# Gate columns of the second block's memory folded into the first values tiles, and the tiles beside the second attention moved up one unit

## The reference, cut to what matters

```
h = modulate(rms_norm_2(x, norm_mix_g), sh1, sc1)
proj = h @ w_in                                   # 1024 x 2832
q_a, k_a, v_a, qk_m, v_m, o_m, gates = split(proj)  # 512, 128, 128, 1024, 512, 512, 16 columns
y_attn = axial_gqa_attention(q_a, k_a, v_a, ...)    # 8 heads, softmax over all 512 keys
qk = silu(conv5(qk_m));  q, k = split(qk)
g = (gates + gate_b).reshape(B, S, 4, 4)            # input and forget gates, forward and backward
h_fw, h_bw = mlstm(q, k, v_m, i, log_sigmoid(f))    # one pass forward, one over the flipped tokens
y_mem = norm(h_fw + h_bw) * norm_g * sigmoid(o_m)
x = x + g1 * concat(y_attn, y_mem) @ w_out
```

## Time and profile before

| | |
|---|---|
| median of 3 runs | 1550.72 us (1549.45 to 1551.03) |
| the profiled execution's own time | 1549.7 us |
| its span, first to last instruction | 1547.9 us |
| PE busy | 1500.0 us (97%), 11612 matmuls |
| PEld, DVE, ACT, POOL busy | 86%, 66%, 42%, 2% |
| mean granted TensorE clock | 0.995 |

### The profile page before, as it was taken

How to read it: one execution, slowest core, us unless ns; L and a number is a source line. 1 busy time by engine, 2 the same in 40 slices (tenths; PEclk the granted TensorE clock), 3 DMA queues, 4 the chain that set the end, 5 groups by cost and what they waited for, 6 DMA issues and landing times.

```text
span 1547.9 us, 27582 instructions
## 1 busy us (share of the span) xinstructions
PE 1500.0 (97%) x11612; PEld 1326.0 (86%) x11612; DVE 1024.9 (66%) x1441; ACT 655.4 (42%) x1052; POOL 23.2 (2%) x20
## 2 busy tenths in 40 slices
PE   7999999999998999999999899999989999999998
PEld 7988878888998999999887667767767999998876
DVE  5533446785446877777656766676688888885454
ACT  5433343433334222122343545546645555554343
POOL 0000000000000000000000011000000000000000
PEclk9999999999999999999999999999999999999999
DMA  5221104452231333332445213110013233222222
GB/s 182 83 83 55 42 3 153 153 173 95 95 109 70 103 137 103 115 124 76 137 148 166 96 49 109 55 35 28 28 55 109 82 110 110 95 98 82 95 95 82
DMA packets 37707, 147.72 MB, mean 95 GB/s; under 512 B 4305, under 2 KB 4433, under 8 KB 27857
## 3 DMA queue, kind: packets, MB, share of 16 engines
q1 hardware_dynamic: 36288, 142.76, 27.2%
q10 hardware_dynamic: 1152, 2.16, 0.4%
q0 software_dynamic: 144, 1.05, 0.2%
HBM read 143.86 MB, written 2.10 MB: 94 GB/s over the span
## 4 chain that ended last, share of the span: by engine, by line
PE 85%; DVE 8%; ACT 4%; issue 2%; ACTq 0%; POOL 0%; DVEq 0%
PE ps L567 19%; PE ps L569 18%; PE ps L568 18%; PE ps L1489 4%; PE ps L1487 4%; PE ps L1488 4%; ACT t L1540 1%; DVE t L2265 1%; PE ps L603 1%; PE ps L604 1%; PE ps L605 1%; PE ps L751 1%; PE ps L1193 1%; PE ps L729 1%; PE ps L1162 1%
## 5 line engine op out<-in xcount | busy, mean ns | idle before, releaser
L567 PE MATMUL ps<-t 128*128 128x258 f32 (+4 forms) x2160 | 688.9, 319 | 23.1 <-DVE t L2313 8.7
L569 PE MATMUL ps<-t 128*128 128x258 f32 (+4 forms) x2160 | 677.2, 313 | 0.0
L568 PE MATMUL ps<-t 128*128 128x258 f32 (+4 forms) x2160 | 675.7, 313 | 0.0
L567 PEld LDWEIGHTS ps<-t 128*128 128x128 f32 (+1 forms) x2160 | 407.3, 189 | 67.4 <-issue 16.8
L569 PEld LDWEIGHTS ps<-t 128*128 128x128 f32 (+1 forms) x2160 | 407.0, 188 | 27.3
L568 PEld LDWEIGHTS ps<-t 128*128 128x128 f32 (+1 forms) x2160 | 407.7, 189 | 23.8
L2265 DVE TENSOR_TENSOR t<-t 128x1024 fp32r<-128x1024 f32 (+2 forms) x121 | 205.6, 1700 | 204.3 <-ACT t L1540 204.2
L1540 ACT ACTIVATE t<-t 128x1024 fp32r<-128x1024 f32 (+2 forms) x121 | 174.0, 1438 | 186.7 <-PE ps L569 173.6
L1489 PE MATMUL ps<-t 128*128 128x256 f32 x504 | 142.6, 283 | 0.0
L1487 PE MATMUL ps<-t 128*128 128x256 f32 x504 | 142.5, 283 | 0.1
L1488 PE MATMUL ps<-t 128*128 128x256 f32 x504 | 141.3, 280 | 0.0
(11 more groups left out here) (324 smaller groups left out, 1785.2 us busy)
## 6 DMA issues: line engine op xcount, KB each, us to landing
t<-in_W SPq DMA_DIRECT2D x75, 1024.0 KB, 4.8
t<-in_W SPq DMA_DIRECT2D x62, 512.0 KB, 3.6
t<-in_W SPq DMA_DIRECT2D x100, 256.0 KB, 4.0
t<-in_W SPq DMA_DIRECT2D x4, 644.0 KB, 3.8
t<-in_XT ACTq DMA_DIRECT2D x8, 264.0 KB, 7.5
out<-t SPq DMA_DIRECT2D x8, 256.0 KB, 2.7
t<-in_ROPE POOLq DMA_DIRECT2D x1, 1024.0 KB, 5.2
t<-in_CONS SPq DMA_DIRECT2D x1, 423.0 KB, 11.3
```

What stands on the lines that cost most here:

```text
L567: pe.matmul(out, wh, xh, start=first, stop=False)
L568: pe.matmul(out, wh, xl, start=False, stop=False)
L569: return pe.matmul(out, wl, xh, start=False, stop=last)
```

## The change

The gates' weight chunk goes. Their 16 columns stand in the first two values chunks (338 columns for 322), so that `v5_first` leaves them, token-major, at columns 322 to 337 of banks 0 to 3. `evac_v5(0, t)` copies them with one more operation into `gtok`, a tile of 4 x 128 columns that GpSimd has zeroed, 4 columns at 0, 32, 64 and 96 of each 128. A new `gate_turn` in unit 0 transposes the four into bank 0, where the gate tile stood before.

Unit u now computes tile f = u+1, and unit 16 none. ScalarE's and VectorE's work on the tiles and the splits are one unit earlier: splits in even units up to 12, the convolution in units 5 to 12. `gate_rows` stays in units 1 to 5, `gate_columns`, `gcol` and `ncol` in unit 8, the steps on `mrow` in units 2, 6 and 7; the columns go through bank 0, and tile f = 10 waits for them.

```diff
-ORDER += [("q2", 0), ("kq", 0), ("q3", 0), ("v5", 0), ("v5", 1), ("gt2", 0), ("o2", 0), ("o2", 1)]
+ORDER += [("q2", 0), ("kq", 0), ("q3", 0), ("v5", 0), ("v5", 1), ("o2", 0), ("o2", 1)]
...
+        gtok = mb[0][:, :].rearrange("p (t n) -> p t n", t=4)
...
         def gq_split(u):
-            return AT["o2", 0] + (0 if u == 0 else (u + 1) // 2) if u == 0 or (u % 2 == 1 and u <= 13) else None
+            return AT["o2", 1] + u // 2 if u % 2 == 0 and u <= 12 else None
...
+        def gates_of(t):
+            return bank(t, 16, off=322).rearrange("p (g c) -> p g c", g=4)
+
+        def gate_slots(t):
+            return gtok[:, t, :].rearrange("p (g c) -> p g c", g=4)[:, :, 0:4]
...
             po.dma_start(rope[:, :, :], ROPE).then_inc(S["d_rope"], 16)
+            po.memset(mb[0][:, :], 0.0).then_inc(S["half"], 1)
...
-                    out, a = bank(t, 322), slice(128 * t, 128 * t + 128)
+                    out, a = bank(t, 338), slice(128 * t, 128 * t + 128)
...
                 if part == 0:
-                    if f == 0:
-                        pe.wait_ge(S["ev_v5_d"], 1)
-                    elif f == 1:
+                    if f == 1:
                         pe.wait_ge(S["ev_v5_a"], 1)
                     elif f == 2:
                         pe.wait_ge(S["gt_a"], 1)
...
-                    if f == 9:
+                    if f == 10:
                         pe.wait_ge(S["gt_d"], 6)
                         pe.wait_ge(S["gt_a"], 5)
...
+            def gate_turn():
+                pe.wait_ge(S["ev_v5_a"], 2)
+                pe.wait_ge(S["ev_v5_d"], 2)
+                for t in range(4):
+                    ins = pe.transpose(bank(0, P, off=128 * t), gtok[:, t, :], C("id"))
+                ins.then_inc(S["mm_gt"], 1)
 
             def gate_columns():
-                pe.wait_ge(S["cv_c"], 3)
+                pe.wait_ge(S["cv_c"], 4)
...
-                            ins = pe.transpose(bank(1, 4, off=c0 + 16 * d + 4 * i), rw[:, 128 * i:128 * i + 128],
+                            ins = pe.transpose(bank(0, 4, off=c0 + 16 * d + 4 * i), rw[:, 128 * i:128 * i + 128],
...
             for u in range(17):
                 if u < 15:
                     gqa_scores(u + 1)
-                beside_attention(u, 0)
                 if u < 16:
+                    beside_attention(u + 1, 0)
                     gqa_turn(u, 0)
+                if u == 0:
+                    gate_turn()
                 if u >= 1:
                     gqa_values(u - 1)
-                beside_attention(u, 1)
                 if u < 16:
+                    beside_attention(u + 1, 1)
                     gqa_turn(u, 1)
...
@@ ScalarE
+                    if c == 0:
+                        ac.wait_ge(S["half"], 2)
+                        ac.activation(gate_slots(t), gates_of(t), ACT.Copy)
...
-            split(AT["gt2", 0])
+            split(AT["o2", 0])
...
+                if u == 1:
+                    beside_attention(0)
                 if u >= 1:
-                    beside_attention(u - 1)
-                if u == 13:
+                    beside_attention(u)
+                if u == 12:
                     split(gq_split(u))
                 if u < 15:
                     gqa_exp(u + 1)
-                if gq_split(u) is not None and u != 13:
+                if gq_split(u) is not None and u != 12:
                     split(gq_split(u))
...
-                if u == 16:
-                    beside_attention(16)
@@ VectorE
+                    if c == 0:
+                        dv.wait_ge(S["half"], 2)
+                        dv.tensor_copy(gate_slots(t), gates_of(t))
...
-            split(AT["gt2", 0])
+            split(AT["o2", 0])
...
-                if u == 5:
+                if u == 4:
                     dv.wait_ge(S["r_y"], 15)
                     for i in range(2):
                         dv.memset(cv[i], 0.0).then_inc(S["cv_z"], 1)
-                if 6 <= u <= 13:
-                    evac_conv(u - 6)
-                if 14 <= u:
-                    evac_v5(1, u - 14)
+                if 5 <= u <= 12:
+                    evac_conv(u - 5)
+                if 13 <= u:
+                    evac_v5(1, u - 13)
...
-                    dv.tensor_copy(gcol[:, :], bank(1, 32)).then_inc(S["gt_d"], 6)
+                    dv.tensor_copy(gcol[:, :], bank(0, 32)).then_inc(S["gt_d"], 6)
```

More of the change, by code:

```diff
@@ L74 @@
 for _i in range(4):
-    _chunk(("v5", _i), 1288)
-_chunk(("gt2", 0), 1024)
+    _chunk(("v5", _i), 1352 if _i < 2 else 1288)
 for _i in range(22):
@@ L97 @@
     FILL_B += [(_n, 2 * _p), (_n, 2 * _p + 1)]
-USED = {("f", 0): ("mm_f", 1), ("gt2", 0): ("mm_gt", 1), ("q2", 0): ("mm_q2", 3), ("kq", 0): ("mm_q2", 7),
+USED = {("f", 0): ("mm_f", 1), ("q2", 0): ("mm_q2", 3), ("kq", 0): ("mm_q2", 7),
         ("q3", 0): ("mm_q2", 8)}
@@ L1227, in beside_attention @@
                     return
-                if part == 0 and (f == 0 or f % 2 == 1):
-                    w = weights(AT["gt2", 0] + (f + 1) // 2, 8)
-                c = slice(0, 128) if f % 2 == 1 or f == 0 else slice(128, 256)
+                if part == 0 and f % 2 == 1:
+                    w = weights(AT["o2", 0] + f // 2, 8)
+                c = slice(0, 128) if f % 2 == 1 else slice(128, 256)
                 for k in range(4 * part, 4 * part + 4):
@@ L1233, in beside_attention @@
                 if part == 1:
-                    ins.then_inc(S["mm_gt"] if f == 0 else S["mm_o2"] if f <= 4 else S["mm_cv"], 1)
+                    ins.then_inc(S["mm_o2"] if f <= 4 else S["mm_cv"], 1)
+            def gate_turn():
[4 more added lines that the diff above has]
+                ins.then_inc(S["mm_gt"], 1)
             def gate_columns():
-                pe.wait_ge(S["cv_c"], 3)
+                pe.wait_ge(S["cv_c"], 4)
                 for d in range(2):
@@ L2053, in _ @@
                     ac.activation(ncol[:, :].rearrange("p (d h i) -> p d i h", d=2, h=4),
-                                  bank(1, 32, off=32).rearrange("p (d i h) -> p d i h", d=2, h=4), ACT.Exp, scale=-1.0
+                                  bank(0, 32, off=32).rearrange("p (d i h) -> p d i h", d=2, h=4), ACT.Exp, scale=-1.0
                                   ).then_inc(S["gt_a"], 5)
@@ L3170, in lay_out @@
     v[:, 128:644].reshape(1024, 4, 129)[:, :, 0:128] = w[:, 1792:2304].reshape(1024, 4, 128)
-    parts["v5"] = v.reshape(2, 4, 128, 2, 322).transpose(3, 0, 2, 1, 4).reshape(4, -1)
+    v = np.concatenate([v[:, 0:322], w[:, 2816:2832], v[:, 322:644]], 1).reshape(2, 4, 128, 660).transpose(0, 2, 1, 3)
+    parts["v5"] = [v[j, :, :, c].reshape(-1) for c in (slice(0, 338), slice(338, 660)) for j in range(2)]
     parts["o2"] = _cols(w[:, 2304:2816], 8, 256)
-    g = np.zeros((1024, 4, 32), np.float32)
-    g[:, :, 0:4] = w[:, 2816:2832].reshape(1024, 4, 4)
-    parts["gt2"] = _cols(g.reshape(1024, 128), 8, 128)
     parts["wo2a"] = _cols(i["w_out_2"][0][0:512], 4, 256)
```

## The result

The changed kernel takes 1556.07 us (median of 5, 1555.77 to 1557.55), before 1550.72: **5.3 us slower**, ratio 1.0036, 95% interval 1.0024 to 1.0049. The forecast was 1553.6, most likely within 0.2%. The time lies in the whole range of the prediction (1549 to 1556.2), but it is a slowdown that can be told from none, and nearly twice the 2.9 us forecast. The profiled execution has a span of 1554.1 us.

What follows compares the result with a forecast made beforehand. VectorE's chain was taken to set the time from unit 4 and ScalarE the end: +1.9 there and +1.0 for the clock make +2.9 on the median 1550.72, 1553.6. The forecast's own range was 1552 to 1555.5, the whole 1549 to 1556.2.

Steps and rivals of the forecast that it cites:

- VectorE sets the time from unit 4 on: Loop units 4 to 8: VectorE's chain sets the pace, M(5) to M(8) at 992.6, 1000.6, 1012.5, 1020.0.
- All four waits: TensorE waits: gate bias in unit 1 0.8, second turn of unit 6 1.3, first of unit 7 1.0, tile f = 10 3.7.
- Ahead of the loop 0.76: Before the loop: wider values matmuls and gate copies start the first scores 0.76 us later, bounds 0.5 to 1.1.
- Removed tile worth nothing where it ends up: End of the loop: the removed tile frees TensorE where it isn't needed, as ScalarE is full there.
- ScalarE's end, +1.9: Behind the last exponentials ScalarE is full; the copy that stood at 1088.43 comes at 1090.3, 1.9 us later.
- the same work follows: Behind ScalarE's copy forecast at 1090.3: the same work as before, no further term.
- The clock: Behind TensorE's pause at tile f = 10: half clock on restart adds 1.0 us, bounds 0 and 1.4.
- rival 4: VectorE's late start also delays units 9 to 12, or the clock falls twice: +5, 1556; chance 0.12.
- The forecast's own range: Whole kernel: 1552 to 1555.5, from start -0.3/+0.3, VectorE chain -1/+1 and clock -1/+0.4.
- Slot parity: Later chunks: one chunk fewer turns their slot parity; costed at nothing, bounds -0.3 to +0.3.
- GpSimd's memset: Memset of 128 x 512 before a power operation ahead of which GpSimd idles 27.9 us: costs nothing.
- Rival 1: Moved tiles don't meet on VectorE, waits of units 6 to 8 don't arise: -4.7, 1546.0; chance 0.12.

Runs made afterwards that it cites:

- the repeat: The changed kernel run again with no edit, also called "changed, again": 1555.97 us against 1550.79 before, ratio 1.0036.
- The fold without the shift: Changed kernel with tiles, splits and convolution in their old units, unit 0 without a tile, its first turned copy ahead of the exponentials: 1546.65 us, ratio 0.9979.
- `mrow`: Changed kernel with ScalarE's `mrow` copies of unit 6 behind the copy of the first turned tile: 1557.41 us, ratio 1.0049 to before.
- odd splits: Changed kernel with splits back in odd units 1 to 11, the last in unit 12: 1553.73 us, ratio 1.0020 to before.
- gate columns in unit 9: Changed kernel with the gate columns one unit later, tile f = 11 waiting for them: 1552.01 us, ratio 0.9998 to before.
- first pause filled: Changed kernel with 15 unused 512-column matmuls in TensorE's 3.8 us pause of unit 9: 1553.32 us, ratio 1.0014 to before.

## Why the prediction was right or wrong

- *VectorE sets the time from unit 4 on; splits, memset, `yal`, `mrow` and gate columns meet in even units*: right. All four waits stand where they were forecast, to 0.3 and the largest to 0.1, and VectorE's starts to 0.2 once the common 0.97 is taken off. Moving only the gate columns gave 3.6 us of loop back.
- *Ahead of the loop 0.76*: 0.75 in the trace. The 16-column copies were cheaper than priced (0.08 from start to start, 939.06 to 939.14 on ScalarE), the matmuls took the rest.
- *Removed tile worth nothing where it ends up*: right. In the shifted order the last unit is the one without a tile, and 2.8 us of idle matmuls there changed nothing. Without the shift and with the first turned copy early, the same removal is worth 4.1 by medians, 3.2 by the traces.
- *ScalarE's end, +1.9*: the mechanism is right, the term too small. With the clock kept up in both places, the loop is 2.8 longer, the rest 1.0 shorter and 0.75 comes ahead: 2.5. ScalarE's own stretch is as forecast (15.49 from 1077.80 to 1093.29, forecast 15.5, before 16.15). Of the missing 0.6, 0.2 is in the loop. The other 0.4 lies behind that copy, where I wrote that "the same work follows": in the three traces without a fall 459.9 us are left from it to the end, before 459.5. The next `prep` copies start 1.70 behind it (1093.29 to 1094.99), before 1.34 (1088.43 to 1089.77).
- *The clock, "so I add 1.0 (bounds 0 and 1.4)"*: this is the step that failed, twice over: one fall was priced too low, and the second was left out. I took the loss from a count of matmuls over one 4 us stretch of the earlier trace rows that began after TensorE had gone on at 479.6, and in that case the half clock lasted only to 482.4, 2.8 us of work. Here it lasted 3.9 us behind the pause, in the repeat 5.9. Measured: 1.8 at the first pause (2.7 in the repeat's loop). And I gave it one fall: the end of the loop, where I wrote that TensorE is freed "where it isn't needed", is itself a TensorE pause of 3.2 us, whose clock I priced only in rival 4 ("or the clock falls twice: +5, 1556", 0.12). That rival is what happened. That its 1556 was hit is luck: by my own terms two falls made 1.9 + 2 x 1.0 = 3.9. What came is 0.75 + 4.59 in the loop - 0.11 in the rest = 5.2, of which 2.7 is the clock (1.8 and 0.9) and 2.5 the rest of the sum.
- *The forecast's own range, 1552 to 1555.5*: its three terms add up to 1551.3 to 1555.3. The result lies above both.
- *Slot parity, GpSimd's memset at nothing*: right. From 1167.56 against 1173.74 to 1479.42 against 1485.61 the distance between the two kernels stays 6.2, and the memset took 0.54 us with 26.8 us of idle GpSimd behind it.
- *Rival 1, TensorE keeps the bound, 1546.0*: fell for the change as made. The fold without the shift comes close to that time (1546.65), but in another order, so this does not bear the rival out.

Left open: why a pause of 3.2 us at the end lowers the clock in four of the six traces of the shifted order that leave it unfilled (changed, again, `mrow`, odd splits) and not in two (gate columns in unit 9, first pause filled). And why it fell behind 1.97 us and not behind 2.29. The medians may carry that 1 us either way, since only one execution of each kernel was traced.

## What to carry to other kernels

Work taken off the busiest engine pays only if the order lets the last dependent chain start earlier; moving everything else up behind it can turn the gain into an idle slot at the end. When steps are shifted against each other, list for every unit what each engine now holds, its waits included, and look for fixed steps (here the gate columns) that land in a unit with a heavy one. Price a long TensorE pause at its length and, with a chance, at the half clock behind it: here a fall cost 1.0 to 2.7 us, and it came behind pauses of 1.97 us and more, though not behind each of them. Look for such pauses also where the forecast says that TensorE has nothing to do.

## What the runs showed of the hardware

- The granted clock stayed at 1.00 behind waits of TensorE of 1.23 and 0.94 us about 5 us apart, behind one of 1.48 and behind one of 2.29 (splits in odd units). It fell at the end of single ones of 1.97 (mean over 4 us 0.57), 2.74 (0.68), 3.63 and 3.81 (0.50). At one of 3.2 it fell in four traces and not in two.
- What a fall cost: 1.8 us at the pause of 3.8, from two kernels that differ by it (2.7 against the repeat), and about 1.0 at that of 3.2, from the rest of seven traces.
- A 16-column copy out of the same PSUM bank ahead of a 322-column one took 0.18 us on ScalarE and 0.17 on VectorE, but the large copy started only 0.08 (939.06 to 939.14) and 0.09 (940.53 to 940.62) behind it.
